# End of a layer in a two-layer hybrid trunk: squares of two of three token chunks added by TensorE, a new order of sums and norms, stores in halves

## Chip, cores and metric

The kernel runs on one core of one Trainium2 chip. The metric is device time of one execution in microseconds (us). The core has five engines that run on their own and meet through semaphores: TensorE (PE, matrix products into the PSUM banks), VectorE (DVE), ScalarE (ACT), GpSimd (POOL) and SyncE (SP, which here only issues transfers).

## The reference, cut to what matters

Two layers run over 1024 prompt tokens and 32 sample tokens. The change lies where a layer ends: the feed-forward result `f` is normed over its 1024 features and added to `x`, and the next layer begins with the norm of the new `x` and its input projection.

```
def rms_norm(x, g):
    xf = x.astype(jnp.float32)
    y = xf * lax.rsqrt(jnp.mean(xf * xf, axis=-1, keepdims=True) + RMS_EPS)
    return (y * g.astype(jnp.float32)).astype(x.dtype)
...
    f = swiglu(rms_norm(x, ng[NORM_FFN_PRE]), w_gu, w_dn)
    x = x + rms_norm(f, ng[NORM_FFN_POST])
    return x, k_keep, v_keep, S_fin, shift_new
...
    P = h @ w_in          # token_mix of the next layer, h = rms_norm(x, ng[NORM_MIX_PRE])
```

## The kernel before, in words

Activations lie with features on the 128 partitions: a tile `[128, 8, 1056]` holds 8 blocks of 128 features for all 1056 tokens. The tokens are worked in three chunks `c` of 352 (0 to 351, 352 to 703, 704 to 1055). `R1` holds `x`; `R2` gathers the feed-forward result and is later reused for squares and for the normed input. Every engine's program is written out by hand, in order; a wait in it holds up whatever is written behind it on that engine. A product of full precision is made of three products of split operands (`WH`, `WL` and `HH`, `HL`), 24 matmuls for one output tile of one chunk.

At the end of a layer each chunk goes through these steps:

- `down(last=True)` on PE makes the last part of the down projection, and `down_sums(c, ...)` on DVE adds it to `R2`, one add for each of 8 blocks. `third_done` tells ACT (`r2_ready`).
- `f_squares(c)` on ACT squares the chunk (2816 elements on each partition) into `SQF`, a single buffer in `TMP`, after waiting until it is free (`fsq_free`). POOL adds the 8 blocks of squares in a tree of three adds into `F_RMS[c]`. `f_stat(c)` on PE, one matmul with a matrix of 1/1024, sums over the partitions into a PSUM bank. The first of them, `f_stat(0)`, stands inside the down projection of chunk 2.
- `root(F_RMS[c], bank)` on ACT makes the reciprocal root out of a logarithm and an exponential (`rms_ready`). `gains_out(c)` multiplies the chunk by the norm's gains, 8 activations.
- `out_normed(c, halves)` on DVE multiplies four blocks by the root and adds them to `R1`, so two `tensor_tensor` for a half. After both halves SP stores the chunk (`x_done`): in layer 0 to `x_spill`, in layer 1 to the output `y`.
- Only behind layer 0: `new_squares(c)` on ACT squares the new `x` in halves, `x_stat(c)` on PE sums them with 8 matmuls, `root(X_RMS[c], ...)` follows, `x_normed` (DVE, 8 operations), `x_high` (ACT, 4 casts) and `x_low` (DVE, 4 subtractions) make the split input, and `opening(c, s)` on PE makes the first two output tiles `s` of the next layer's projection for the chunk, 24 matmuls each. `evac` on ACT copies them out. `lo(0)` and `lo(1)` on DVE finish the split of the two first weight tiles, which `down_split` on ACT begins.

Of the kernel before, what the change touches and what calls it, by code (L numbers as in the profile page):

```python
# [24 lines left out]
ALU = mybir.AluOpType  # L25
# [6 lines left out]
CH = 3  # L32
# [83 lines left out]
def build(nc, io, ctx):  # L116
# [36 lines left out]
    def S(name):  # L153
        if name in ("first_psum", "second_psum"):
            name = "product_of_" + name[:-5] + "_tile"
        elif name.endswith("_psum"):
            name = "product_for_vector" if name in for_vector else "product_for_scalar"
        if name not in sems:
            sems[name] = ctx.enter_context(nc.semaphore(name))
        return sems[name]  # L160

    def give(e, *names):
        for name in names:
            e.sem_inc(S(name), 1)

    def bank(b, a=0, z=512):
        return PS[:, b * 512 + a:b * 512 + z]
# [17 lines left out]
    def chunk(c):  # L185
        return slice(c * CW, (c + 1) * CW)
# [185 lines left out]
    MEM_KV = MIX[:, 14 * ROW + 2560 + MEM:14 * ROW + 2560 + MEM + 4 * 512].rearrange("p (b t) -> p b t", b=4)  # L372


    SQF = tflat[:, 0:DB * CW].rearrange("p (b t) -> p b t", b=DB)
    F_RMS = [SIDE[:, T + 2 + c % 2 * CW:T + 2 + (c % 2 + 1) * CW] for c in range(CH)]
    X_RMS = [SIDE[:, T + 2 + 2 * CW:T + 2 + 3 * CW], tflat[:, DB * CW:(DB + 1) * CW], SIDE[:, T + 2 + 2 * CW:T + 2 + 3 * CW]]
    X_BANK, F_BANKS = 6, (5, 7, 7)
    DOWN_BANKS = [6, 7, 0, 1, 2, 3, 4, 5]


# [21 lines left out]
    def _(e):  # L403
# [12 lines left out]
        for l in range(DEPTH):  # L416
# [141 lines left out]
                w8(0, io["w_in"], l + 1, R0 + 3 * R_WIDTH)  # L558
                w8(1, io["w_in"], l + 1, R0 + 3 * R_WIDTH + P)
            for c in range(CH):  # L560
                e.wait_ge(S("x_done"), 1)
                e.sem_inc(S("x_done"), -1)
                if l < DEPTH - 1:
                    e.dma_start(x_spill[:, :, chunk(c)], R1[:, :, chunk(c)]).then_inc(S("x_spilled"), 16)
                else:
                    e.dma_start(io["y"][:, :, chunk(c)], R1[:, :, chunk(c)]).then_inc(S("y_stored"), 16)
            if l < DEPTH - 1:
                e.wait_ge(S("x_spilled"), 48)
                e.sem_inc(S("x_spilled"), -48)
                give(e, "r1_free")  # L570
        e.wait_ge(S("y_stored"), 48)


    @block.gpsimd
    def _(e):
# [21 lines left out]
        for l in range(DEPTH):  # L597
# [132 lines left out]
            def pool_settled(ins):  # L730

                ins.then_inc(S("pool_done"), 1)
                e.wait_ge(S("pool_done"), 1)
                e.sem_inc(S("pool_done"), -1)

            for c in range(CH):
                e.wait_ge(S("fsq_ready"), 1)
                e.sem_inc(S("fsq_ready"), -1)
                pool_settled(e.tensor_tensor(SQF[:, 0:4, :], SQF[:, 0:4, :], SQF[:, 4:8, :], ALU.add))
                pool_settled(e.tensor_tensor(SQF[:, 0:2, :], SQF[:, 0:2, :], SQF[:, 2:4, :], ALU.add))  # L740
                pool_settled(e.tensor_tensor(F_RMS[c], SQF[:, 0, :], SQF[:, 1, :], ALU.add))
                give(e, "fsq_free", "fsq_sum")
        barrier(e, "pool")


# [1 line left out]
    def _(e):  # L747
        def claim(*banks):
            for b in banks:
                e.wait_ge(S(f"bank{b}"), 1)  # L750
                e.sem_inc(S(f"bank{b}"), -1)  # L751
# [29 lines left out]
                         lambda k, p: H[p][:, k, c * cw:(c + 1) * cw], DB).then_inc(S(name), 1)  # L781

        def x_stat(c):
            claim(X_BANK)
            for h in range(2):
                e.wait_ge(S("xsq_ready"), 1)
                e.sem_inc(S("xsq_ready"), -1)
                for b in range(4 * h, 4 * h + 4):
                    ins = e.matmul(bank(X_BANK, 0, CW), mean, R2[:, b, chunk(c)], start=(b == 0), stop=(b == DB - 1))
            ins.then_inc(S("var_psum"), 1)  # L790

        def f_stat(c):
            e.wait_ge(S("fsq_sum"), 1)
            e.sem_inc(S("fsq_sum"), -1)
            claim(F_BANKS[c])
            e.matmul(bank(F_BANKS[c], 0, CW), mean, F_RMS[c], start=True, stop=True).then_inc(S("var_psum"), 1)

        def opening(c, s):

            if c == 0:  # L800
                e.wait_ge(S(f"w_ready{s}"), 1)
                e.sem_inc(S(f"w_ready{s}"), -1)
            claim(3 * s + c)
            for k in range(DB):
                if s == 0 and k % 2 == 0:
                    e.wait_ge(S("h_ready"), 1)
                    e.sem_inc(S("h_ready"), -1)
                for w, h in ((WH, HH), (WL, HH), (WH, HL)):
                    ins = e.matmul(bank(3 * s + c, 0, CW), w[:, s, k * P:(k + 1) * P], h[:, k, chunk(c)],
                                   start=(k == 0 and w is WH and h is HH), stop=(k == DB - 1 and h is HL))  # L810
            ins.then_inc(S(("first_psum", "second_psum")[s]), 1)
# [5 lines left out]
        for l in range(DEPTH):  # L817
            if l == 0:
                opening(0, 0)
                x_stat(1)  # L820
            else:
                x_stat(1)
                opening(0, 0)
            opening(0, 1)
            opening(1, 0)
            x_stat(2)
            opening(1, 1)
            opening(2, 0)
            opening(2, 1)
# [674 lines left out]
                gate_up()  # L1504
            down(last=True)
            f_stat(1)
            if l < DEPTH - 1:
                x_stat(0)
            f_stat(2)
        barrier(e, "pe")  # L1510


# [2 lines left out]
    def _(e):  # L1515
# [49 lines left out]
        for b in range(8):  # L1565
            give(e, f"bank{b}")

        give(e, "sq_free", "sq_free", "ot_free", "sc_free", "sc_free", "fsq_free")
        roots_ahead()
        split(0)  # L1570
        split(1)
        for l in range(DEPTH):
            PRM = PRMS[:, l * PRM_COLS:(l + 1) * PRM_COLS]
            vec = lambda at, n, j: PRM[:, at + 4 * n + j:at + 4 * n + j + 1]
            if l == 0:
                for c in range(CH):
                    e.wait_ge(S(f"x_full{c}"), 16)
                    e.sem_inc(S(f"x_full{c}"), -16)
                    x_squares(c, 0)
                    x_squares(c, 1)  # L1580
                    root(X_RMS[c], X_BANK)
                    x_high(c, 0, 1, 2, 3)

            def raw(m=P):
# [144 lines left out]
            def settled(ins):  # L1729

                ins.then_inc(S("act_done"), 1)
                e.wait_ge(S("act_done"), 1)
                e.sem_inc(S("act_done"), -1)
# [512 lines left out]
            def f_squares(c):  # L2246
                e.wait_ge(S("r2_ready"), 1)
                e.sem_inc(S("r2_ready"), -1)
                e.wait_ge(S("fsq_free"), 1)
                e.sem_inc(S("fsq_free"), -1)  # L2250
                settled(e.activation(SQF, R2[:, :, chunk(c)], ACT.Square))
                give(e, "fsq_ready")

            def gains_out(c):
                for b in range(DB):
# [22 lines left out]
            f_squares(1)  # L2278
            root(F_RMS[0], F_BANKS[0])
            gains_out(1)  # L2280
            root(F_RMS[1], F_BANKS[1])
            new_squares(0)
            f_squares(2)
            down_split(0)
            down_split(1)
            if l < DEPTH - 1:
                root(X_RMS[0], X_BANK)
                new_squares(1)
                x_high(0, 0, 1, 2, 3)
            gains_out(2)  # L2290
            root(F_RMS[2], F_BANKS[2])
            if l < DEPTH - 1:
                root(X_RMS[1], X_BANK)
                x_high(1, 0, 1, 2, 3)
                new_squares(2)
                root(X_RMS[2], X_BANK)
                x_high(2, 0, 1, 2, 3)
        barrier(e, "act")

# [2 lines left out]
    def _(e):  # L2302
# [35 lines left out]
        for l in range(DEPTH):  # L2338
# [693 lines left out]
            def third_done():  # L3032

                settled(e.memset(ST[:, 0:1], 0.0))
                give(e, "r2_ready")

            def out_normed(c, *halves):
                for h in halves:
                    if h == 0:
                        wait_for("rms_ready")  # L3040
                        wait_for("gained")
                    b = slice(4 * h, 4 * h + 4)
                    r1, r2 = R1[:, b, chunk(c)], R2[:, b, chunk(c)]
                    settled(e.tensor_tensor(r2, r2, F_RMS[c].unsqueeze(1).broadcast_to([P, 4, CW]), ALU.mult))
                    settled(e.tensor_tensor(r1, r1, r2, ALU.add))  # L3045
                    if l < DEPTH - 1:
                        give(e, "r1_ready")
                if 1 in halves:
                    give(e, "x_done")

            half(0)
# [4 lines left out]
            third_done()  # L3056
            down_sums(2, *range(4))
            out_normed(0, 0)
            down_sums(2, 4, 5)
            out_normed(0, 1)  # L3060
            down_sums(2, 6, 7)
            third_done()
            out_normed(1, 0, 1)
            if l < DEPTH - 1:
                NEXT = PRMS[:, (l + 1) * PRM_COLS:(l + 2) * PRM_COLS]
                lo(0)
                lo(1)
                x_normed(NEXT, 0, 0, 1, 2, 3)
                x_low(0, 0, 1, 2, 3)
                out_normed(2, 0, 1)  # L3070
                for c in (1, 2):
                    x_normed(NEXT, c, 0, 1, 2, 3)
                    x_low(c, 0, 1, 2, 3)
            else:
                out_normed(2, 0, 1)
# [53 lines left out]
```

## Time and profile before

| what | value |
|---|---|
| median of 3 runs | 4000.9 us (3997.28 to 4009.68) |
| profiled execution, its own time | 3997.58 us |
| its span, first to last instruction | 3995.6 us |
| mean granted TensorE clock | 0.934 |
| PE busy | 3551.0 us (89%) |
| DVE busy | 1765.8 us (44%) |
| ACT busy | 1300.1 us (33%) |
| POOL busy | 162.7 us (4%) |

The profile is one execution; all places are in us from the start of its span. Shares of busy time are means over the whole span: the two stretches that the change touches (about 1958 to 2050, and 3937 to the end) are read by themselves. A matmul of 352 columns with plain float32 operands shows as two records.

### The profile page before, as it was taken

The page shows a single profiled execution, that of the slowest core. Times are in us where ns is not written, and L with a number is a line of the kernel's source. Part 1 is how long each engine was busy: PE and PEld are TensorE (multiplying, and loading weights), DVE is VectorE, ACT ScalarE, POOL GpSimd, SP SyncE. Part 2 cuts the span into 40 slices and gives each one's busy share as a digit, 9 for nine tenths or more (in the row PEclk, how much of TensorE's full clock was granted, in tenths as well). Part 3 has the DMA queues.
Part 4 walks back from the last instruction along what each step waited for, and adds up shares of the span by engine and source line. Part 5 has one row for each costly group of instructions (what it writes and reads, how often), then busy time and mean ns, then how long its engine had stood idle before and what let it go on. Part 6 is the DMA issues. An engine that isn't in the chain of part 4 may idle for free. (4 is left out here: it accounts for less than half of the span.)

```text
span 3995.6 us, 84425 instructions
## 1 busy us (share of the span) xinstructions
PE 3551.0 (89%) x32662; PEld 3280.0 (82%) x32662; DVE 1765.8 (44%) x2693; ACT 1300.1 (33%) x2505; POOL 162.7 (4%) x188
## 2 busy tenths in 40 slices
PE   6999689869888999999889976998689799999996
PEld 5988367758878999999879864777588699999996
DVE  3254456524554343333443534555345633333334
ACT  3344445323452111111333434443235521111113
POOL 0010000000100000000200100000001000000002
PEclk8999789969999999999989987999799999999998
DMA  2221210117631111111121222001276211111111
GB/s 86 61 70 66 88 45 27 70 39 264 214 124 32 48 43 46 42 52 43 47 70 57 65 68 97 21 26 73 74 249 233 80 43 42 47 47 42 47 47 54
DMA packets 240704, 298.79 MB, mean 75 GB/s; under 512 B 26616, under 2 KB 195952, under 8 KB 239504
## 3 DMA queue, kind: packets, MB, share of 16 engines
q1 hardware_dynamic: 224368, 227.83, 18.0%
q0 software_dynamic: 16032, 66.75, 4.4%
q8 instruction: 209, 3.42, 0.4%
q14 instruction: 95, 0.78, 0.1%
HBM read 228.91 MB, written 65.63 MB: 74 GB/s over the span
## 5 line engine op out<-in xcount | busy, mean ns | idle before, releaser
L767 PE MATMUL PS<-HH,WH 128*128 128x352 f32 (+2 forms) x3584 | 1190.9, 332 | 66.7 <-PEq L751 66.1
L767 PE MATMUL PS<-HH,WL 128*128 128x352 f32 (+2 forms) x3584 | 1164.0, 325 | 0.0
L767 PE MATMUL PS<-HL,WH 128*128 128x352 f32 (+2 forms) x3584 | 1162.6, 324 | 0.0
L767 PEld LDWEIGHTS PS<-HH,WH 128*128 128x128 f32 x3584 | 684.7, 191 | 84.7 <-issue 81.0
L767 PEld LDWEIGHTS PS<-HH,WL 128*128 128x128 f32 x3584 | 684.7, 191 | 2.9 <-issue 0.6
L767 PEld LDWEIGHTS PS<-HL,WH 128*128 128x128 f32 x3584 | 682.4, 190 | 0.0
L2307 DVE TENSOR_TENSOR WL<-WRAW,WH 128x1024 fp32r<-128x1024 f32 x192 | 236.8, 1234 | 672.6 <-DVEq L2306 672.6
L1517 ACT CAST WH<-WRAW 128x1024 fp32r<-128x1024 f32 x216 | 226.3, 1049 | 631.1 <-ACTq L1526 585.1
L1487 PE MATMUL PS<-GH,WH 128*128 128x352 f32 x1056 | 340.2, 322 | 0.0
L1487 PE MATMUL PS<-GL,WH 128*128 128x352 f32 x1056 | 339.5, 322 | 0.0
L1487 PE MATMUL PS<-GH,WL 128*128 128x352 f32 x1056 | 339.5, 322 | 0.0
L3017 DVE TENSOR_TENSOR R<-R,PS 128x352 f32<-128x352 f32 x432 | 199.9, 517 | 145.4 <-DVEq L3011 145.1
L1517 ACT COPY MIX<-PS 128x512 f32<-128x512 f32 (+3 forms) x250 | 130.5, 525 | 345.7 <-ACTq L1737 199.2
L1487 PEld LDWEIGHTS PS<-GH,WL 128*128 128x128 f32 x1056 | 198.3, 188 | 0.2
L1487 PEld LDWEIGHTS PS<-GH,WH 128*128 128x128 f32 x1056 | 198.3, 188 | 0.2
L1487 PEld LDWEIGHTS PS<-GL,WH 128*128 128x128 f32 x1056 | 198.3, 188 | 0.0
L2194 ACT ACTIVATE TMP<-PS 128x352 f32<-128x352 f32 x132 | 61.3, 465 | 400.1 <-ACTq L2193 400.0
L2969 DVE TENSOR_TENSOR TMP<-TMP,PS 128x352 f32<-128x352 f32 x132 | 68.8, 521 | 275.1 <-DVEq L2965 275.1
L2545 DVE COPY_PREDICATED TMP<-CST,PS 128x512 f32<-128x512 uint32 (+1 forms) x162 | 109.8, 696 | 127.1 <-DVEq L2516 127.0
L1517 ACT COPY TMP<-PS 128x256 f32<-128x256 f32 (+2 forms) x252 | 104.4, 444 | 159.9 <-ACTq L1737 138.3
L1517 ACT CAST GH<-TMP 128x352 fp32r<-128x352 f32 x132 | 63.8, 485 | 255.4 <-ACTq L2206 255.4
L1517 ACT COPY R<-PS 128x384 f32<-128x384 f32 (+3 forms) x166 | 73.4, 442 | 186.8 <-ACTq L1534 111.0
(324 smaller groups left out, 4870.9 us busy)
## 6 DMA issues: line engine op xcount, KB each, us to landing
WRAW<-in_w_gate_up SPq DMA_DIRECT2D x88, 512.0 KB, 3.7
W<-split_dram SPq DMA_DIRECT2D x48, 512.0 KB, 4.5
WRAW<-in_w_down SPq DMA_DIRECT2D x44, 512.0 KB, 3.4
WH<-split_dram SPq DMA_DIRECT2D x40, 512.0 KB, 3.7
WL<-split_dram SPq DMA_DIRECT2D x40, 512.0 KB, 4.6
WRAW<-in_w_in SPq DMA_DIRECT2D x38, 512.0 KB, 3.8
raw_dram<-MIX SPq DMA_DIRECT2D x24, 528.0 KB, 2.6
R<-raw_dram SPq DMA_DIRECT2D x24, 512.0 KB, 4.6
```

The costliest lines, as they stand in the source:

```text
L767: ins = e.matmul(out, lhs(k, wp), rhs(k, xp), start=first, stop=(k == n - 1 and xp == 1))
L1487: ins = e.matmul(bank(b, 0, CW), w[:, k, m * P:(m + 1) * P], g[:, k, chunk(c)], start=(k == 0 and w is WH and g is GH), stop=(k == 1 and g ...
L1517: return e.copy(dst, src)
L2194: e.activation(TMP[:, 0, chunk(c)], bank(c, 0, CW), ACT.Silu).then_inc(S("act_done"), 1)
L2307: e.tensor_tensor(WL[:, slot, :], WRAW[:, slot, :], WH[:, slot, :].bitcast(F32), ALU.subtract).then_inc(S("dve_done"), 1)
L2545: e.copy_predicated(x[:, 0:n, :], bits(m).unsqueeze(1).broadcast_to([P, n, CHUNK]), bank(b, 0, n * CHUNK).rearrange("p (g t) -> p g t", t= ...
L2969: e.tensor_tensor(TMP[:, 1, chunk(c)], TMP[:, 0, chunk(c)], bank(3 + c, 0, CW), ALU.mult).then_inc(S("dve_done"), 1)
L3017: e.tensor_tensor(R2[:, m, chunk(c)], R2[:, m, chunk(c)], bank(b, 0, CW), ALU.add).then_inc(S(f"bank{b}"), 1)
```

## The change

For chunks 1 and 2 the tree of adds on POOL is gone: each chunk has a buffer of squares of its own, in `MIX`, and `f_stat(c)` sums the 8 blocks by 8 matmuls into one PSUM bank. Chunk 0 keeps POOL's tree. The wait for the single buffer is gone. DVE makes the whole of chunk 2's down sums before the second half of chunk 0's output norm; the output norm of chunk 2 stands ahead of the next layer's norm of chunk 0. ACT squares chunk 2 ahead of the second root. PE makes `f_stat(2)` ahead of `x_stat(0)`, and `x_stat(2)` ahead of the first opening. Stores go by halves of a chunk (four blocks). Some roots and sums have other buffers and banks.

```
-    SQF = tflat[:, 0:DB * CW].rearrange("p (b t) -> p b t", b=DB)
+    SQF = [MIX[:, DB * T + c * DB * CW:DB * T + (c + 1) * DB * CW].rearrange("p (b t) -> p b t", b=DB) for c in range(CH)]
-    X_BANK, F_BANKS = 6, (5, 7, 7)
+    X_BANKS, F_BANKS = (6, 7, 6), (5, 7, 5)
...
             for c in range(CH):
+                for b in (slice(0, 4), slice(4, 8)):
+                    e.wait_ge(S("x_done"), 1)
...
+                        e.dma_start(x_spill[:, b, chunk(c)], R1[:, b, chunk(c)]).then_inc(S("x_spilled"), 16)
...
         def f_stat(c):
-            e.wait_ge(S("fsq_sum"), 1)
-            e.sem_inc(S("fsq_sum"), -1)
+            name = "fsq_sum" if c == 0 else "fsq_whole"
+            e.wait_ge(S(name), 1)
+            e.sem_inc(S(name), -1)
             claim(F_BANKS[c])
-            e.matmul(bank(F_BANKS[c], 0, CW), mean, F_RMS[c], start=True, stop=True).then_inc(S("var_psum"), 1)
+            rows = [F_RMS[0]] if c == 0 else [SQF[c][:, b, :] for b in range(DB)]
+            for n, row in enumerate(rows):
+                ins = e.matmul(bank(F_BANKS[c], 0, CW), mean, row, start=(n == 0), stop=(n == len(rows) - 1))
+            ins.then_inc(S("var_psum"), 1)
...
             else:
                 x_stat(1)
+                x_stat(2)
                 opening(0, 0)
             opening(0, 1)
             opening(1, 0)
-            x_stat(2)
+            if l == 0:
+                x_stat(2)
...
             f_stat(1)
+            f_stat(2)
             if l < DEPTH - 1:
                 x_stat(0)
-            f_stat(2)
...
             f_squares(1)
             root(F_RMS[0], F_BANKS[0])
             gains_out(1)
+            f_squares(2)
             root(F_RMS[1], F_BANKS[1])
             new_squares(0)
-            f_squares(2)
+            gains_out(2)
             down_split(0)
             down_split(1)
...
             down_sums(2, *range(4))
             out_normed(0, 0)
-            down_sums(2, 4, 5)
+            down_sums(2, *range(4, 8))
+            third_done()
             out_normed(0, 1)
-            down_sums(2, 6, 7)
-            third_done()
             out_normed(1, 0, 1)
             if l < DEPTH - 1:
                 NEXT = PRMS[:, (l + 1) * PRM_COLS:(l + 2) * PRM_COLS]
                 lo(0)
                 lo(1)
-                x_normed(NEXT, 0, 0, 1, 2, 3)
-                x_low(0, 0, 1, 2, 3)
                 out_normed(2, 0, 1)
-                for c in (1, 2):
+                for c in range(CH):
                     x_normed(NEXT, c, 0, 1, 2, 3)
                     x_low(c, 0, 1, 2, 3)
```

On ACT, at the end of layer 0, the order before is this (L2251 is `f_squares`, L2257 `gains_out`, L1551 and L1555 the two steps of `root`, L1546 `new_squares`, L1517 a copy or cast):

```order
L2251 ACTIVATE TMP<-R 128x2816
L1551 ACTIVATE SIDE<-PS,CST 128x352
L1555 ACTIVATE SIDE<-SIDE 128x352
L2257 ACTIVATE R<-R,PRMS 128x352 x8
L1551 ACTIVATE SIDE<-PS,CST 128x352
L1555 ACTIVATE SIDE<-SIDE 128x352
L1546 ACTIVATE R<-R 128x4x352 x2
L2251 ACTIVATE TMP<-R 128x2816
L1517 CAST WH<-WRAW 128x1024 x2
L1551 ACTIVATE SIDE<-PS,CST 128x352
L1555 ACTIVATE SIDE<-SIDE 128x352
L1546 ACTIVATE R<-R 128x4x352 x2
```

The same place of the changed kernel, from `f_squares(1)` on (the lines' numbers are higher by 5 to 7):

```order
L2256 ACTIVATE MIX<-R 128x2816
L1558 ACTIVATE SIDE<-PS,CST 128x352
L1562 ACTIVATE SIDE<-SIDE 128x352
L2262 ACTIVATE R<-R,PRMS 128x352 x8
L2256 ACTIVATE MIX<-R 128x2816
L1558 ACTIVATE SIDE<-PS,CST 128x352
L1562 ACTIVATE SIDE<-SIDE 128x352
L1553 ACTIVATE R<-R 128x4x352 x2
L2262 ACTIVATE R<-R,PRMS 128x352 x8
L1524 CAST WH<-WRAW 128x1024 x2
L1558 ACTIVATE TMP<-PS,CST 128x352
L1562 ACTIVATE TMP<-TMP 128x352
```

Chunk 2's squares moved ahead of the second root, and chunk 2's gains and third output root moved ahead of the next layer's first root.

On PE, the end of layer 0 before, from the last matmul of the down projection (L1487) on, with `f_stat` (L796), `x_stat` (L789) and the first opening (L809):

```order
L1487 MATMUL PS<-GL,WH 128x352
L796 MATMUL PS<-SIDE,CST 128x352
L789 MATMUL PS<-R,CST 128x352 x8
L796 MATMUL PS<-SIDE,CST 128x352
L789 MATMUL PS<-R,CST 128x352 x8
L809 MATMUL PS<-HH,WH 128x352
```

And of the changed kernel:

```order
L1494 MATMUL PS<-GL,WH 128x352
L800 MATMUL PS<-MIX,CST 128x352 x16
L790 MATMUL PS<-R,CST 128x352 x24
L814 MATMUL PS<-HH,WH 128x352
L814 MATMUL PS<-HH,WL 128x352
```

Both output sums of 8 matmuls now stand ahead of all three sums of the next norm, and all of these ahead of the first opening.

On DVE, from the second half of chunk 1's output norm (L3044, L3045) on, before: `lo` (L2307), `x_normed` (L2319), `x_low` (L2327).

```order
L3044 TENSOR_TENSOR R<-R,SIDE 128x4x352
L3045 TENSOR_TENSOR R<-R 128x4x352
L2307 TENSOR_TENSOR WL<-WRAW,WH 128x1024 x2
L2319 SCALAR_TENSOR_TENSOR R<-R,PRMS,SIDE 128x352 x8
L2327 TENSOR_TENSOR HL<-R,HH 128x2x352 x4
L3044 TENSOR_TENSOR R<-R,SIDE 128x4x352
L3045 TENSOR_TENSOR R<-R 128x4x352
```

And of the changed kernel:

```order
L3048 TENSOR_TENSOR R<-R,SIDE 128x4x352
L3049 TENSOR_TENSOR R<-R 128x4x352
L2311 TENSOR_TENSOR WL<-WRAW,WH 128x1024 x2
L3048 TENSOR_TENSOR R<-R,TMP 128x4x352
L3049 TENSOR_TENSOR R<-R 128x4x352
L3048 TENSOR_TENSOR R<-R,TMP 128x4x352
L3049 TENSOR_TENSOR R<-R 128x4x352
L2323 SCALAR_TENSOR_TENSOR R<-R,PRMS,SIDE 128x352 x8
L2331 TENSOR_TENSOR HL<-R,HH 128x2x352 x4
```

The output norm of chunk 2, four operations, passed the next layer's norm and split of chunk 0, twelve operations.

## Rows read from the trace of the kernel before

**Rows 1.** PE by stretch (us from start): length, busy (instructions), granted clock, DMA share, GB/s.

```profile
1983.00:1985.00 2.00, 1.51 (x2) 0.50 0.00 0
2009.00:2017.00 8.00, 7.64 (x49) 1.00 0.00 0
2017.00:2026.00 9.00, 0.00 (x0) 0.67 0.43 160
2060.00:2150.00 90.00, 89.44 (x560) 0.99 0.21 60
```

**Rows 2.** Timeline of POOL, layer 0's end: start, length, operation, idle before.

```profile
1974.20 3.23 POOL L739 TENSOR_TENSOR TMP<-TMP 128x1408 f32<-128x1408 f32 x1 [3.10 <-POOLq L738]
...
1980.62 2.09 POOL L741 TENSOR_TENSOR SIDE<-TMP 128x352 f32<-128x352 f32 x1 [0.18 <-POOLq L734]
```

**Rows 3.** Timeline of ACT, layer 0's end and layer 1's start.

```profile
1962.01 2.55 ACT L2251 ACTIVATE TMP<-R 128x2816 f32<-128x2816 f32 x1 [5.80 <-ACTq L2250]
...
1971.35 2.56 ACT L2251 ACTIVATE TMP<-R 128x2816 f32<-128x2816 f32 x1 [2.65 <-ACTq L2250]
1974.19 0.56 ACT L1551 ACTIVATE SIDE<-PS,CST 128x352 f32<-128x352 f32 x1 [0.28 <-ACTq L1550]
...
1975.34 3.93 ACT L2257 ACTIVATE R<-R,PRMS 128x352 f32<-128x352 f32 x8
...
1986.01 2.63 ACT L1546 ACTIVATE R<-R 128x1408 f32<-128x1408 f32 x2
1988.54 2.54 ACT L2251 ACTIVATE TMP<-R 128x2816 f32<-128x2816 f32 x1
1991.44 2.00 ACT L1517 CAST WH<-WRAW 128x1024 fp32r<-128x1024 f32 x2 [0.36 <-ACTq L1526]
...
2049.04 0.52 ACT L1517 COPY SIDE<-PS 128x320 f32<-128x320 f32 x2 [4.73 <-ACTq L1534]
```

**Rows 4.** Timeline of DVE, the same stretch.

```profile
1961.58 0.06 DVE L3034 MEMSET ST<- 128x1 f32 x1
...
1969.01 0.06 DVE L3034 MEMSET ST<- 128x1 f32 x1
...
1974.50 0.52 DVE L3030 TENSOR_TENSOR R<-R,PS 128x352 f32<-128x352 f32 x1 [0.43 <-DVEq L2516]
1975.69 3.22 DVE L3044 TENSOR_TENSOR R<-R,SIDE 128x1408 f32<-128x1408 f32 x1 [0.68 <-DVEq L2516]
...
2001.65 1.22 DVE L2307 TENSOR_TENSOR WL<-WRAW,WH 128x1024 fp32r<-128x1024 f32 x1 [0.44 <-DVEq L2306]
...
2013.52 1.62 DVE L3044 TENSOR_TENSOR R<-R,SIDE 128x1408 f32<-128x1408 f32 x1 [2.93 <-DVEq L2516]
...
2018.93 1.62 DVE L3045 TENSOR_TENSOR R<-R 128x1408 f32<-128x1408 f32 x1
...
2038.28 4.06 DVE L2319 SCALAR_TENSOR_TENSOR R<-R,PRMS,SIDE 128x352 f32<-128x352 f32 x8 [10.01 <-DVEq L2316]
2042.25 3.29 DVE L2327 TENSOR_TENSOR HL<-R,HH 128x704 fp32r<-128x704 f32 x4
```

**Rows 5.** Timeline of PE: output sums (L796), sums of the next norm (L789).

```profile
1971.60 0.83 PE L796 MATMUL PS<-SIDE,CST 128*128 128x352 f32 x2 [1.31 <-PEq L751]
1983.21 1.51 PE L796 MATMUL PS<-SIDE,CST 128*128 128x352 f32 x2 [5.05 <-PEq L751]
2001.93 7.08 PE L789 MATMUL PS<-R,CST 128*128 128x352 f32 x16
2031.86 4.89 PE L789 MATMUL PS<-R,CST 128*128 128x352 f32 x16
```

**Rows 6.** Timeline of DVE, layer 1's end: first and last output-norm operations.

```profile
3954.35 3.22 DVE L3044 TENSOR_TENSOR R<-R,SIDE 128x1408 f32<-128x1408 f32 x1 [0.68 <-DVEq L2516]
...
3987.89 1.62 DVE L3045 TENSOR_TENSOR R<-R 128x1408 f32<-128x1408 f32 x1
```

**Rows 7.** Half a microsecond within the last store, columns as in rows 1.

```profile
3992.00:3992.50 0.50, 0.00 (x0) 0.50 1.07 400
```

More of the change, by code:

```diff
@@ L372, in build @@
     MEM_KV = MIX[:, 14 * ROW + 2560 + MEM:14 * ROW + 2560 + MEM + 4 * 512].rearrange("p (b t) -> p b t", b=4)
-    SQF = tflat[:, 0:DB * CW].rearrange("p (b t) -> p b t", b=DB)
-    F_RMS = [SIDE[:, T + 2 + c % 2 * CW:T + 2 + (c % 2 + 1) * CW] for c in range(CH)]
+    SQF = [MIX[:, DB * T + c * DB * CW:DB * T + (c + 1) * DB * CW].rearrange("p (b t) -> p b t", b=DB) for c in range(CH)]
+    F_RMS = [SIDE[:, T + 2:T + 2 + CW], SIDE[:, T + 2 + CW:T + 2 + 2 * CW], tflat[:, 0:CW]]
     X_RMS = [SIDE[:, T + 2 + 2 * CW:T + 2 + 3 * CW], tflat[:, DB * CW:(DB + 1) * CW], SIDE[:, T + 2 + 2 * CW:T + 2 + 3 * CW]]
-    X_BANK, F_BANKS = 6, (5, 7, 7)
+    X_BANKS, F_BANKS = (6, 7, 6), (5, 7, 5)
     DOWN_BANKS = [6, 7, 0, 1, 2, 3, 4, 5]
@@ L560, in _ @@
             for c in range(CH):
[L561 to L566, printed above, removed]
+                for b in (slice(0, 4), slice(4, 8)):
+                    e.wait_ge(S("x_done"), 1)
+                    e.sem_inc(S("x_done"), -1)
+                    if l < DEPTH - 1:
+                        e.dma_start(x_spill[:, b, chunk(c)], R1[:, b, chunk(c)]).then_inc(S("x_spilled"), 16)
+                    else:
+                        e.dma_start(io["y"][:, b, chunk(c)], R1[:, b, chunk(c)]).then_inc(S("y_stored"), 16)
             if l < DEPTH - 1:
-                e.wait_ge(S("x_spilled"), 48)
-                e.sem_inc(S("x_spilled"), -48)
+                e.wait_ge(S("x_spilled"), 96)
+                e.sem_inc(S("x_spilled"), -96)
                 give(e, "r1_free")
-        e.wait_ge(S("y_stored"), 48)
+        e.wait_ge(S("y_stored"), 96)
     @block.gpsimd
@@ L734, in pool_settled @@
                 e.sem_inc(S("pool_done"), -1)
[L736 to L742, printed above, removed]
+            e.wait_ge(S("fsq_ready"), 1)
+            e.sem_inc(S("fsq_ready"), -1)
+            sq = SQF[0]
+            pool_settled(e.tensor_tensor(sq[:, 0:4, :], sq[:, 0:4, :], sq[:, 4:8, :], ALU.add))
+            pool_settled(e.tensor_tensor(sq[:, 0:2, :], sq[:, 0:2, :], sq[:, 2:4, :], ALU.add))
+            pool_settled(e.tensor_tensor(F_RMS[0], sq[:, 0, :], sq[:, 1, :], ALU.add))
+            give(e, "fsq_sum")
         barrier(e, "pool")
@@ L783, in x_stat @@
         def x_stat(c):
-            claim(X_BANK)
+            claim(X_BANKS[c])
             for h in range(2):
@@ L788, in x_stat @@
                 for b in range(4 * h, 4 * h + 4):
-                    ins = e.matmul(bank(X_BANK, 0, CW), mean, R2[:, b, chunk(c)], start=(b == 0), stop=(b == DB - 1))
+                    ins = e.matmul(bank(X_BANKS[c], 0, CW), mean, R2[:, b, chunk(c)], start=(b == 0), stop=(b == DB - 1))
             ins.then_inc(S("var_psum"), 1)
         def f_stat(c):
-            e.wait_ge(S("fsq_sum"), 1)
-            e.sem_inc(S("fsq_sum"), -1)
+            name = "fsq_sum" if c == 0 else "fsq_whole"
+            e.wait_ge(S(name), 1)
+            e.sem_inc(S(name), -1)
             claim(F_BANKS[c])
-            e.matmul(bank(F_BANKS[c], 0, CW), mean, F_RMS[c], start=True, stop=True).then_inc(S("var_psum"), 1)
+            rows = [F_RMS[0]] if c == 0 else [SQF[c][:, b, :] for b in range(DB)]
+            for n, row in enumerate(rows):
+                ins = e.matmul(bank(F_BANKS[c], 0, CW), mean, row, start=(n == 0), stop=(n == len(rows) - 1))
+            ins.then_inc(S("var_psum"), 1)
         def opening(c, s):
@@ L822, in _ @@
                 x_stat(1)
+                x_stat(2)
                 opening(0, 0)
@@ L825, in _ @@
             opening(1, 0)
-            x_stat(2)
+            if l == 0:
+                x_stat(2)
             opening(1, 1)
@@ L1506, in _ @@
             f_stat(1)
+            f_stat(2)
             if l < DEPTH - 1:
                 x_stat(0)
-            f_stat(2)
         barrier(e, "pe")
@@ L1566, in _ @@
             give(e, f"bank{b}")
-        give(e, "sq_free", "sq_free", "ot_free", "sc_free", "sc_free", "fsq_free")
+        give(e, "sq_free", "sq_free", "ot_free", "sc_free", "sc_free")
         roots_ahead()
@@ L1580, in _ @@
                     x_squares(c, 1)
-                    root(X_RMS[c], X_BANK)
+                    root(X_RMS[c], X_BANKS[c])
                     x_high(c, 0, 1, 2, 3)
@@ L2248, in f_squares @@
                 e.sem_inc(S("r2_ready"), -1)
[L2249 to L2252, printed above, removed]
+                settled(e.activation(SQF[c], R2[:, :, chunk(c)], ACT.Square))
+                give(e, "fsq_ready" if c == 0 else "fsq_whole")
             def gains_out(c):
@@ L2280, in _ @@
             gains_out(1)
+            f_squares(2)
             root(F_RMS[1], F_BANKS[1])
             new_squares(0)
-            f_squares(2)
+            gains_out(2)
             down_split(0)
             down_split(1)
[L2286 to L2290, printed above, removed]
             root(F_RMS[2], F_BANKS[2])
             if l < DEPTH - 1:
-                root(X_RMS[1], X_BANK)
+                root(X_RMS[0], X_BANKS[0])
+                new_squares(1)
+                new_squares(2)
+                x_high(0, 0, 1, 2, 3)
+                root(X_RMS[1], X_BANKS[1])
                 x_high(1, 0, 1, 2, 3)
-                new_squares(2)
-                root(X_RMS[2], X_BANK)
+                root(X_RMS[2], X_BANKS[2])
                 x_high(2, 0, 1, 2, 3)
@@ L3047, in out_normed @@
                         give(e, "r1_ready")
-                if 1 in halves:
                     give(e, "x_done")
@@ L3058, in _ @@
             out_normed(0, 0)
-            down_sums(2, 4, 5)
+            down_sums(2, *range(4, 8))
+            third_done()
             out_normed(0, 1)
-            down_sums(2, 6, 7)
-            third_done()
             out_normed(1, 0, 1)
@@ L3067, in _ @@
                 lo(1)
-                x_normed(NEXT, 0, 0, 1, 2, 3)
-                x_low(0, 0, 1, 2, 3)
                 out_normed(2, 0, 1)
-                for c in (1, 2):
+                for c in range(CH):
                     x_normed(NEXT, c, 0, 1, 2, 3)
```

## The prediction

> **What bounds the kernel now.** I read the stretches of TensorE first. From 2060 on it is busy 89.44 of 90 us at full clock, so what comes earlier at the start of layer 1 comes earlier to the end, as long as TensorE stays the bound; just ahead of that it stands idle, 9 us from 2017 to 2026 alone [rows 1]. So the end of layer 0 and the start of layer 1 are a chain of small steps on four engines, and so is the end of layer 1, behind which nothing runs but the last store. I followed that chain in the timelines of the single engines. The reader is to see how late chunk 2 is: its squares start at 1988.54 [rows 3], its output norm runs from 2013.52 to 2020.55 [rows 4], the sum for its next norm starts at 2031.86, behind an opening [rows 5], its next norm at 2038.28 after 10.01 us without work for VectorE [rows 4], and the copy of its first opened tile at 2049.04 [rows 3]. I take this last place as the end of the first stretch. In layer 1 the end is VectorE's last addition, 3987.89 + 1.62 = 3989.51 [rows 6], and 6.1 us of store up to the end of the span at 3995.6.
>
> **Layer 0, step by step.** Each new place is the place of the releaser plus a duration from a row.
>
> Chunk 1's squares waited 2.65 us for the one buffer and started at 1971.35 [rows 3]. With their own buffer they follow the memset that ends chunk 1's sums (1969.01 [rows 4]) by 0.43, as in chunk 0 (1961.58 [rows 4] to 1962.01 [rows 3]): 1969.44 to 1972.0. The sum of chunk 0 on TensorE stays where it is, ending at 1971.60 + 0.83 = 1972.43 [rows 5], and the first root, which started at 1974.19 behind those squares, starts near 1972.6. A root takes 1.25 (1974.19 to just behind 1975.34 [rows 3]); so 1973.85, then chunk 1's gains, 3.95, to 1977.8.
>
> VectorE finishes block 3 of chunk 2 at 1975.02 [rows 4] and begins chunk 0's output norm at 1975.25. The first operation took 3.22 there while POOL added (1974.20 on [rows 2]), and 1.62 where POOL was at rest [rows 4]. POOL's second tree is gone, so I take a half from 2013.52 to 2020.55, where two halves took 7.03 [rows 4]: 3.4, to 1978.65. Four adds at about 0.45 (0.52 for one alone [rows 4]) follow, to 1980.8. Chunk 2's squares start at 1981.2, not 1988.54, and end at 1983.75.
>
> TensorE ends the down projection at 1983.21 - 5.05 = 1978.16 [rows 5]. Eight matmuls from the squares' buffer do not occur before; the nearest rows are the sums of the next norm, also eight matmuls of 352 columns: 4.89 at full clock, 7.08 where the clock was half at first [rows 5]. Half throughout would be twice 4.7, 9.4. The first output sum stands right behind the projection at full clock, so I take 4.89: to 1983.0. The second waits for chunk 2's squares, 1.1 us idle, little less than the 1.31 after which one matmul still took 0.83 [rows 5]; again 4.89, 1984.1 to 1989.0. Before, POOL's tree alone took from 1974.20 to 1982.71 for chunk 1 [rows 2].
>
> ScalarE then has no pause: second root to 1985.3, squares of the new chunk 0 (2.63) to 1987.9, gains of chunk 2 (3.95) to 1991.85, two casts (0.36 + 2.00 [rows 3]) to 1994.2, third root to 1995.5. Here the stall goes: VectorE, done with chunk 0 at 1984.7 and with chunk 1 (1985.55 + 7.03) at 1992.6, waits for the casts, makes its two splits (1.22 and a gap of 0.44 each [rows 4]) to 1996.4, and begins chunk 2's output norm at 1996.8 instead of 2013.52; it ends at 2003.85.
>
> ScalarE makes the next norm's first root to 1996.7 and chunk 1's new squares to 1999.3; TensorE, idle for about 4 us after chunk 0's sum (1989.0 to 1993.9), begins chunk 1's sum at 1998.1. I take the 7.08 of the same sum before [rows 5]: 2005.2. Chunk 2's new squares end at 2005.5, its sum at 2009.9, the gate for the first opening now. The other gate, the first quarter of VectorE's split input, is open by 2009.2: 2003.85, 0.45, 4.06 for the norm, a quarter of 3.29 [rows 4]. So the first opening goes from near 2008.6 to 2009.9, a loss of 1.3 that costs nothing, since the openings of chunk 1 waited until 2026 anyhow.
>
> From there work is packed. Two openings took 7.64 [rows 1], 3.82 each; chunks 0 and 1 last until 2025.2. VectorE meanwhile makes norm and split of chunks 1 and 2 at 0.45 + 4.06 + 3.2 each: chunk 2's first quarter is ready at 2024.6, just in time. Chunk 2's first opening ends at 2029.0 and its copy is at 2029.1, where it was 2049.04: **19.9 us**. The weights that SP loads behind its wait for the spills come earlier too: the last half is handed over at 2003.85 instead of 2020.55, the load is needed at 2029.8. If that cover of some 20 us were gone, each microsecond would count in full.
>
> **Layer 1.** The steps lie 3954.35 - 1975.69 = 1978.66 later [rows 4, 6]. Chunk 2's squares end at 3962.4, the output sums at 3961.6 and 3967.7, the second root at 3963.95; chunk 1's output norm runs from 3964.2 to 3971.2, the third root is there by 3969.1, and chunk 2's norm ends at 3978.5, 11.0 ahead of 3989.51. The store of a chunk is 128 x 8 x 352 x 4 = 1.44 MB, 3.6 us at the 400 GB/s of [rows 7]; half of it is still to go at VectorE's end, the first half has left 3.5 us before. That saves 1.8: **12.8 us** in all.
>
> A page speaks against halves: the Trainium skill (DMA: Bandwidth & Descriptors, Anatomy of one DMA) gives each transfer a fixed part of some 2.0 us besides its bytes at 436 GB/s, so that two halves pay it twice. By that estimate the last half takes 2.0 + 1.65 us against 2.0 + 3.3, and the sum would be 0.15 us higher; the trace agrees on a part that does not shrink, 6.1 less 3.6. No run here shows a half store yet.
>
> Bounds of that store: nothing saved (+1.8, if both halves land together) and 1.8. Bounds of the sums on TensorE: all at 4.89 the first opening would be limited by the split input at 2009.2, 0.7 sooner; chunk 1's and 2's sums both at 9.4 put it to 2016.9, 7 later. The other edits (banks, buffers in other tiles, no wait for a free buffer, the halved spill) I put at nothing: an operation on 352 columns does not depend on its tile in these rows, and SP has no other work there; at most 1 us either way.
>
> **Sum.** 3997.6 (the profiled execution's own time) - 19.9 - 12.8 = 3964.9. The median of the runs shown is 3.3 above that execution; going a third of the way, I predict 3966.
>
> **Rivals.** *TensorE at half clock in both sums' stretches.* The clock does fall in such pauses: 1.51 for one matmul at 1983.21, at the 1.2 GHz level, after 5.05 us idle [rows 1, 5]. If it fell in the change's new pauses too and all sums took 9.4: output sums to 1987.5 and 1996.9, the three others to 2025.1, the first opening 15.2 later; in layer 1 the last norm starts at 3977.1, 5.7 later. 3964.9 + 20.9 = 3985.8. Against it: no pause of over 1.4 us stands ahead of the output sums, and the sum at 2001.93 rose to full clock within itself (7.08, not 9.4 [rows 5]). The Trainium skill (TensorE: Matmul & The Clock Gate, Part 1) says that the array's default is the throttled state and that activity releases it; by that rule only the sums after pauses pay, and the trace agrees.
>
> *Slower: the half clock holds through the openings.* They stand in the same queue, behind all sums. Five openings at twice 3.82 add 19.1: 4004.9, and every further tile of 72 matmuls 11.5. It turns into a loss once about three openings run at half clock besides all the sums. Against it: from 2009 to 2017 two openings ran at 1.00 [rows 1].
>
> *The next layer swallows its part.* If the loads behind the spills, or VectorE's work on the first tiles, set the start of the long products, only layer 1's 12.8 stays: 3984.8. Against it: TensorE is full from 2060 on [rows 1], and everything between the copy at 2049.04 and there hangs on that copy.
>
> *The change does not do what it says.* ScalarE, in order, is then late by as much as POOL was, and the time is 3997.6. It would need 33 us of new waits; ScalarE's work between 1969 and 1996 holds only the 4 us that VectorE waits and splits.
>
> **Chances.** Forecast 0.79; half clock 0.08; swallowed 0.06; slower 0.03; nothing 0.04. The forecast's own range is 3960 to 3974: the bounds above and the runs' spread. For 8 in 10 I reach a little into the rivals: 3958 to 3979. Within 0.3% means 12 us here, what a measurement of this kernel can hardly tell from no change. Faster by more: the forecast, the swallowed case and half of the first rival, 0.89; within: 0.08; slower by more: 0.03.
>
> **What the profile will show.** If right: no POOL adds for chunks 1 and 2; sixteen matmuls behind the down projection in about 11 us at clock 1.00; the first operation of the output norm at 1.6, not 3.2; chunk 2's output norm from 1997; the first opening near 2010 and from there no idle TensorE of more than 2 us until 2029; VectorE's last addition near 3978 and the end under 4.5 us behind it. Wrong, if the sums on TensorE show 9 us, if ScalarE's third root comes after 1998, or if the first opening starts after 2017.

## The result and the profile after

The changed kernel takes 3960.27 us (median of 4 runs, 3954.13 to 3967.17) against 3999.09 us for the kernel before (4 runs). The medians differ by 38.8 us. The ratio on record, worked out from the runs of both, is 0.989, 95% interval 0.9873 to 0.9907, so the change is faster by some 39 to 44 us; the forecast of 3966 lay 35 us below the median of 4000.9 that it went from. Five more runs gave a ratio of 0.9894 (0.9877 to 0.9911). The profiled execution takes 3954.13 us.

The trace is best read in four parts. The first end goes from the memset behind chunk 0's sums of layer 0 (1961.58 in [rows 4]) to the copy of chunk 2's first opened tile (2049.04 in [rows 3]), the second from the same memset of layer 1 to the end of the span. Ahead of the first end, and between the two, both kernels do the same work in the same order; only the bank of a sum at the start of layer 0 differs. The lengths in this table are differences of such places in the two traces.

| part, us | before | after | difference |
|---|---|---|---|
| up to layer 0's end | 1961.58 | 1955.06 | -6.52 |
| layer 0's end | 87.46 | 66.63 | -20.83 (19.9 forecast) |
| layer 1 between the ends | 1891.18 | 1888.92 | -2.26 |
| layer 1's end | 55.38 | 41.89 | -13.49 (12.8 forecast) |

The first and the third row of this one pair are not a result: the runs below show how much executions of one kernel differ there.

Timeline of VectorE in the changed kernel, layer 0's end, answering to [rows 4]. In brackets stand the idle time ahead of an operation and what ended it; DVEq, ACTq and PEq are the engines' own sequencers, in which the waits stand:

```profile
1955.06 0.06 DVE L3038 MEMSET ST<- 128x1 f32 x1
...
1968.25 1.62 DVE L3048 TENSOR_TENSOR R<-R,SIDE 128x1408 f32<-128x1408 f32 x1
...
1978.54 1.63 DVE L3048 TENSOR_TENSOR R<-R,SIDE 128x1408 f32<-128x1408 f32 x1 [0.98 <-DVEq L2520]
...
1989.56 1.63 DVE L3048 TENSOR_TENSOR R<-R,TMP 128x1408 f32<-128x1408 f32 x1 [0.56 <-DVEq L2520]
...
1997.14 4.05 DVE L2323 SCALAR_TENSOR_TENSOR R<-R,PRMS,SIDE 128x352 f32<-128x352 f32 x8 [0.46 <-DVEq L2320]
2001.12 3.29 DVE L2331 TENSOR_TENSOR HL<-R,HH 128x704 fp32r<-128x704 f32 x4
2004.33 4.04 DVE L2323 SCALAR_TENSOR_TENSOR R<-R,PRMS,TMP 128x352 f32<-128x352 f32 x8
2008.30 3.28 DVE L2331 TENSOR_TENSOR HL<-R,HH 128x704 fp32r<-128x704 f32 x4
2011.51 4.05 DVE L2323 SCALAR_TENSOR_TENSOR R<-R,PRMS,SIDE 128x352 f32<-128x352 f32 x8
```

The first operation of the output norm takes 1.62, not 3.22; chunk 2's norm starts 34.5 behind the memset, where it started 51.9 behind it; and behind the operation at 1978.54 no pause exceeds 0.56 up to the end of chunk 2's split at 2018.7. The 10 us pause ahead of chunk 2's next norm is gone. From 1978.54 on VectorE sets the pace of this stretch; ahead of that it still waits for TensorE's down projection.

Timelines of ScalarE and of TensorE in the changed kernel, same stretch, answering to [rows 3, 5]:

```profile
1962.84 2.55 ACT L2256 ACTIVATE MIX<-R 128x2816 f32<-128x2816 f32 x1 [0.74 <-ACTq L2255]
...
1974.20 2.55 ACT L2256 ACTIVATE MIX<-R 128x2816 f32<-128x2816 f32 x1 [3.23 <-ACTq L2255]
1977.03 0.56 ACT L1558 ACTIVATE SIDE<-PS,CST 128x352 f32<-128x352 f32 x1 [0.28 <-ACTq L1557]
...
1986.43 0.54 ACT L1558 ACTIVATE TMP<-PS,CST 128x352 f32<-128x352 f32 x1
...
2021.69 0.52 ACT L1524 COPY SIDE<-PS 128x320 f32<-128x320 f32 x2 [4.15 <-ACTq L1541]
```

```profile
1971.32 4.89 PE L800 MATMUL PS<-MIX,CST 128*128 128x352 f32 x16
1977.17 4.97 PE L800 MATMUL PS<-MIX,CST 128*128 128x352 f32 x16 [0.96 <-PEq L752]
1981.98 4.90 PE L790 MATMUL PS<-R,CST 128*128 128x352 f32 x16
1990.22 11.40 PE L790 MATMUL PS<-R,CST 128*128 128x352 f32 x32 [3.34 <-PEq L788]
```

Both output sums of eight matmuls run at full clock, at 4.9 each. The two sums of the next norm behind the pause of 3.34 take 11.4 together, 1.6 more than twice 4.9, and the granted clock is near its lower level at their start. PE by stretch, columns as in [rows 1]:

```profile
1990.20:1994.00 3.80, 3.78 (x7) 0.55 0.00 0
1994.00:1998.00 4.00, 4.00 (x15) 1.00 0.51 188
```

The memset behind chunk 0's sums and the last operation of VectorE in layer 1, answering to [rows 6]:

```profile
3910.61 0.06 DVE L3038 MEMSET ST<- 128x1 f32 x1
...
3946.92 1.62 DVE L3049 TENSOR_TENSOR R<-R 128x1408 f32<-128x1408 f32 x1
```

The latter ends 3.9 ahead of the end of the span (3952.5); before, 6.1.

### The profile page after: what moved, and what is told of

Read it like the earlier page. It is cut to its first block and busy times, and to the rows that moved or that the text cites. A ratio compares the mean times of both kernels' runs of the same rounds, so it can differ in the third digit from the quotient of the medians.

```text
span 3952.5 us, 84510 instructions
## 1 busy us (share of the span) xinstructions
PE 3549.4 (90%) x32718; PEld 3277.7 (83%) x32718; DVE 1754.3 (44%) x2693; ACT 1300.6 (33%) x2505; POOL 130.5 (3%) x176
```

## Experiments

**The kernel before again**, for the parts that no edit touched.

> The kernel before, unchanged. Between the two profiles 6.5 us of the difference lie ahead of the end of layer 0 and 2.3 us between the two ends, where both kernels have the same instructions. Theory (these 8.8 us are what one execution differs from the next by, not the change): this profile reaches the memset behind chunk 0's sums of layer 0 at a place that differs from 1961.58 by several us, the length from the opened tile's copy to the same memset of layer 1 differs from 1891.2 by some us, and the time stands at 1.000 +- 0.002. Rival (the change makes the unchanged stretches shorter, by the bank of a sum at the start or the place of a buffer): the memset stands within 1 us of 1961.6 and the second stretch within 1 us of 1891.2.

Ratio 1.0001 (0.9979 to 1.0024). The 27 runs of before beside this and the next three kernels went from 3984.68 to 4022.62 us. The profile reaches the memset at 1954.59, 7.0 sooner than the first one, and layer 1 between the ends takes 1899.1, 7.9 longer. The two ends take 87.52 and 55.39, within 0.1 of the first. So the ends repeat; the other parts don't, and a single pair of profiles can't be subtracted there.

**Stores of whole chunks** (the edit on SP and the matching counts):

```
-                for b in (slice(0, 4), slice(4, 8)):
...
+                e.dma_start(x_spill[:, :, chunk(c)], R1[:, :, chunk(c)]).then_inc(S("x_spilled"), 16)
```

> The changed kernel with stores of whole chunks. Theory: from VectorE's last addition to the end of the span 6.1 us instead of the 4.0 of the changed kernel, nothing else in the two ends moves (70.1 us from chunk 0's sums to the copy of chunk 2's opened tile in layer 0): some 2 us slower than the changed kernel, ratio to before about 0.990. Rival (the spill in halves lets the next layer's weights come sooner and counts in layer 0): the layer 0 stretch grows by 1 us or more as well.

Ratio 0.992 (0.9895 to 0.9945). Layer 0's end 66.72, layer 1's 43.77; from VectorE's last addition to the end 6.12. The half store is worth 1.9 us, all at the very end. The spill in halves is worth nothing.

**POOL adds again, new order kept:**

```
-            rows = [F_RMS[0]] if c == 0 else [SQF[c][:, b, :] for b in range(DB)]
+            rows = [F_RMS[c]]
...
+            for c in range(CH):
+                e.wait_ge(S("fsq_ready"), 1)
```

> The changed kernel, but POOL adds the squares of all chunks again, with the new order and a buffer for each chunk. Theory (order and sums share the gain, the order having most of it in layer 0): the output norm's first operation takes 3.2 us again, chunk 2's output norm starts 3 to 4 us later in layer 0 and 6 us later in layer 1, so about 9 us slower than the changed kernel, ratio 0.992. Rival (the sums on TensorE are the whole gain): both ends are back near the lengths of before, 91 and 55 us, ratio 1.0. Rival (the order is the whole gain): within 2 us of the changed kernel.

Ratio 0.9937 (0.9913 to 0.9961). Layer 0's end 73.29, layer 1's 47.20: 6.7 and 5.3 longer than in the changed kernel. Chunk 1's output norm in this kernel, on VectorE, against POOL's adds for chunk 2:

```profile
1992.54 3.53 DVE L3048 TENSOR_TENSOR R<-R,SIDE 128x1408 f32<-128x1408 f32 x1 [0.97 <-DVEq L2520]
1996.22 2.86 DVE L3049 TENSOR_TENSOR R<-R 128x1408 f32<-128x1408 f32 x1
```

```profile
1991.05 3.54 POOL L741 TENSOR_TENSOR MIX<-MIX 128x1408 f32<-128x1408 f32 x1 [4.62 <-POOLq L739]
1994.77 2.83 POOL L742 TENSOR_TENSOR MIX<-MIX 128x704 f32<-128x704 f32 x1 [0.18 <-POOLq L735]
```

VectorE's 1.62 becomes 3.53 and 2.86 while POOL adds. The first ends 1.5 behind the end of POOL's first add (1994.59), the second (1999.08) 1.5 behind the end of its second (1997.60). So the two seem to take turns. GpSimd's adds suffer too: the second one takes 2.83 here, and 1.71 for chunk 0, where VectorE's adds beside it take one operand from PSUM. The direction and the contention are as expected, and neither rival holds; layer 0's part was expected at 3 to 4 and is 6.7, layer 1's at 6 and is 5.3.

**Only the sums on TensorE, old order** (`f_stat`, buffers and POOL's part as in the change, chunk 2's buffer in `TMP`):

```
+            rows = [F_RMS[0]] if c == 0 else [SQF[c][:, b, :] for b in range(DB)]
```

> The kernel before with the sums of chunks 1 and 2 on TensorE, buffers of their own (chunk 2's in TMP), and nothing else changed: old order, whole stores. Theory: layer 1's end is shorter by about 9.6 us, since VectorE's last addition comes that much sooner; layer 0's by only about 7 of the 20.8, since chunk 2's output norm still stands behind chunk 0's next norm and its next sum behind an opening: ratio about 0.996. Rival (the sums are the whole gain): 20 us in layer 0, ratio 0.991. Rival (only the order counts): ratio 1.000.

Ratio 0.996 (0.9939 to 0.9981). The ends take 79.38 and 47.31, each 8.1 shorter than before: 7 and 9.6 were expected. In layer 0 VectorE still waits ahead of chunk 2's output norm:

```profile
2001.18 1.62 DVE L3046 TENSOR_TENSOR R<-R,TMP 128x1408 f32<-128x1408 f32 x1 [2.94 <-DVEq L2518]
```

So the sums alone give 8.1 of the 20.8 us in layer 0. The order with POOL's sums gave 14.2 of them; the two overlap a little.

**The changed kernel again.**

> The changed kernel again. Up to here the two ends of the trace are 20.8 and 13.5 us shorter than before, 34.3 in all, and they repeat to 0.1 us, while the unchanged stretches differ by up to 13 us between executions. Theory (only the ends count): ratio 34.3 / 4001 below one, 0.9914, with the ends at 66.6 and 41.9 us again. Rival (the first four runs' 0.989 holds something that the ends don't show): 0.989 or below.

Ratio 0.9894 (0.9877 to 0.9911), 42 us, not the 34 of the ends. The ends are 67.10 and 41.94, within 0.5 of the first profile. The theory that only the ends count, 0.9914, fell just outside the interval.

**Chunk 2's next sum behind an opening again:**

```
             else:
                 x_stat(1)
-                x_stat(2)
                 opening(0, 0)
             opening(0, 1)
             opening(1, 0)
-            if l == 0:
-                x_stat(2)
+            x_stat(2)
```

> The changed kernel with the sum of chunk 2's next norm behind the first opening of chunk 1 again, as before. Theory: VectorE, which works without pause up to chunk 2's next norm in the changed kernel, gets a pause of some 8 us ahead of it (the sum starts near the end of that opening, takes 5 us, the root 1.3), so layer 0's end is 74 to 76 us instead of 66.6 and layer 1's stays at 41.9; ratio 0.9935. Rival (the place of this sum doesn't count, since the first opening is held up by it as much as it gains): 66 to 67 us.

Ratio 0.9922 (0.9907 to 0.9938). Layer 0's end 78.53, 11.9 longer (7.4 to 9.4 expected), layer 1's 41.93. The wait ahead of chunk 2's next norm is back on VectorE:

```profile
2025.45 4.06 DVE L2321 SCALAR_TENSOR_TENSOR R<-R,PRMS,SIDE 128x352 f32<-128x352 f32 x8 [11.23 <-DVEq L2318]
```

This one move in TensorE's order carries more than half of layer 0's gain, as long as the others stand.

**Chunk 2's last down sums late again** (`down_sums(2, 4, 5)`, `out_normed(0, 1)`, `down_sums(2, 6, 7)` as before).

> The changed kernel with the last down sums of chunk 2 behind the second half of chunk 0's output norm again, in the pieces of before. Theory: chunk 2's squares start some 3.6 us later, ScalarE makes the second root behind them, and VectorE waits that much longer: layer 0's end 70.3, layer 1's 45.5 us instead of 66.6 and 41.9. Rival (the pause is taken up by the wait for the second root that stands there anyhow): both ends within 1 us of the changed kernel.

One run, 3969.9 us. Ends 71.27 and 45.98, 4.6 and 4.1 longer (3.7 and 3.6 expected). Chunk 1's output norm waits for the second root, which ScalarE makes at 1987.75, behind chunk 2's squares:

```profile
1989.25 1.63 DVE L3048 TENSOR_TENSOR R<-R,SIDE 128x1408 f32<-128x1408 f32 x1 [4.62 <-DVEq L2520]
```

**Moved on:** chunk 0's output sum one block later, one weight split earlier, the last half stored in quarters.

```
-                        if by_block and i == 3:
+                        if by_block and i == 5:
...
             out_normed(0, 1)
+            if l < DEPTH - 1:
+                lo(0)
             out_normed(1, 0, 1)
```

> The changed kernel with three further moves: chunk 0's output sum one block later in the down projection (behind block 2 instead of 1), the first of the two weight splits ahead of chunk 1's output norm (its cast ahead of chunk 2's squares), and the last half of the last chunk added and stored in two quarters. Theory (VectorE's chain bounds both ends): TensorE's wait of 1.2 us for POOL goes, about 0.9 us in each end; the split fills a pause of 1.0, about 0.5 in layer 0; the quarter saves 0.7 at the end: ends of 65.2 and 40.3 us, 3 us below the changed kernel, ratio to before 0.9907. Rival (the pauses only move on): ends as in the changed kernel.

Ratio 0.989 (0.9872 to 0.9908), which its runs can't tell from the changed kernel's. Its ends are 65.37 and 40.39, 1.3 and 1.5 shorter, as expected. It is the shortest version by the ends. The 0.9907 expected lies inside the interval too.

**Where the other 7 to 8 us are.** In the three profiles of before the part up to layer 0's end takes 1957.1 in the mean, in the two of the changed kernel 1957.0. Layer 1 between the ends takes 1895.0 and 1884.7. Over all 13 traces it takes 1891.2 to 1902.3 in the five with the old number of matmuls on TensorE ahead of it, and 1880.4 to 1891.0 in the eight with 14 more. Cutting all traces at ScalarE's table loads showed one stretch of layer 1 that no edit touches, 73.2 us before and 66.1 after. PE by stretch, columns as in [rows 1], in the kernel before (the whole, and its last part) and in the changed kernel:

```profile
2579.45:2652.67 73.22, 67.08 (x1581) 0.92 0.11 35
2635.00:2652.67 17.67, 14.50 (x286) 0.68 0.01 3
```

```profile
2554.06:2620.14 66.08, 62.43 (x1593) 1.00 0.12 39
```

Before, the granted clock falls to its lower level in the last part; after, it stays at 1.00 all through. Just ahead of the low part TensorE stands still for 1.49 us, and the profile names nothing that it waited for ("issue"); timeline of PE in the kernel before:

```profile
2640.07 0.21 PE L1089 MATMUL PS<-R,TMP 64*64 64x64 f32 x1 [1.49 <-issue]
```

The pause stood in every kernel with the old number of matmuls on TensorE up to there, and in none of those with 14 more. Two kernels test whether that number matters. The first is the kernel before with 14 unused matmuls.

> The kernel before with 14 matmuls more on TensorE at the start of layer 1, between two openings, where it stands idle for 9 us; their sums go to a free bank and are not used. So TensorE's program of layer 1 lies behind as many more instructions as in the changed kernel, while the ends keep the old work. The question is one stretch of layer 1 that no edit touched, between two table loads of ScalarE: 73.2, 72.3 and 73.0 us in the three kernels with the old number of matmuls, with a pause of 1.5 to 1.8 us of TensorE 60 us in, for which the profile names no releaser, and half clock behind it; 65.9 to 66.4 us without that pause in the seven kernels with 14 more. Theory (where TensorE's program lies decides that pause): 66 us here too, no such pause, and the time about 5 to 8 us below before, ratio 0.998 to 0.9985, layer 0's end within 3 us of 87.5. Rival (the pause hangs on when the work comes, and the earlier ends moved it): 73 us and ratio 1.000.

The edit, at the start of layer 1:

```
             opening(0, 1)
+            if l > 0:
+                claim(7)
+                for n in range(14):
+                    ins = e.matmul(bank(7, 0, CW), mean, R1[:, 0, chunk(0)], start=True, stop=True)
+                ins.then_inc(S("bank7"), 1)
             opening(1, 0)
```

Ratio 0.9977 (0.9956 to 0.9997): the kernel before becomes some 9 us faster (1 to 18) by 14 matmuls that nobody uses. Layer 0's end is 85.53, 1.9 shorter than 87.46. There is no pause in the stretch:

```profile
2573.87:2639.53 65.66, 61.86 (x1585) 1.00 0.13 39
```

The second is the changed kernel with 14 left out, so that layer 1 works on other numbers.

> The changed kernel with 14 of the 24 matmuls of the next norm's sums at layer 0's end left out (7 of 8 blocks for chunks 1 and 2, so layer 1 works on other numbers), so that TensorE's program of layer 1 lies where it lay before, with the short ends. Theory (the program's place decides): the stretch is 73 us again with the pause of 1.5 us or more, ratio 0.991 or above, though the sums left out make layer 0's end no longer than 66.7. Rival (timing decides): 66 us, ratio 0.989.

The edit leaves out 7 of 8 blocks of two sums:

```
+                blocks = range(7, 8) if short else range(4 * h, 4 * h + 4)
...
+                x_stat(1, short=True)
+                x_stat(2, short=True)
```

The stretch is long again, with the pause, though it starts 602 us behind the memset of layer 0's end, nearly as early as in the changed kernel (599):

```profile
2567.76:2640.29 72.53, 66.97 (x1585) 0.93 0.11 35
```

```profile
2627.84 0.21 PE L1099 MATMUL PS<-R,TMP 64*64 64x64 f32 x1 [1.22 <-issue]
```

Its ratio, 0.9893 (0.9865 to 0.9922), is open to both expectations. Layer 0's end was 69.23 and not 66.7 or less: without those matmuls the granted clock was 0.50 from 2012.80 to 2018.40, over the start of the openings.

Last, the kernel before a third time.

> The kernel before once more, for the same stretch: by the theory 72 to 73 us and the pause again, as in the two executions so far; by the rival that the pause comes by chance in a single execution, 66 us in some of them.

One run, 3993.88 us: the stretch 71.0, the pause 1.77. The ends 86.78 and 55.42. In three executions of before, then, the pause stood each time; with the 14 unused matmuls and in the changed kernel it was absent. The number of matmuls ahead makes it come and go. When the work comes does not: counted from that memset the stretch starts at 618 in before and 602 with the 14 left out, both with the pause, and at 613 with the 14 unused ones, between them, without it.

The traces say more than the word "issue". In all five traces with the pause, 22084 records of TensorE's matmuls stand ahead of it. In all 13 traces together TensorE has 65 pauses of over 0.9 us without a named releaser, and each ends 1.2 to 1.6 us behind the end of a 16 KB packet of the transfer queue that the page lists as "instruction" (before: packet from 2637.56 to 2638.81, TensorE goes on at 2640.07). Of 245 waits as long with a named releaser, in the same parts of the traces, only 2 end so. So these pauses go with the delivery of instructions. No run changed that delivery by itself.

The number ahead is not all, though. Two pauses of the same kind (1.6 to 2.1 us) stand in the matching stretch of layer 0 in two kernels, the one with POOL's adds in the new order and the one with 14 matmuls left out (72.9 and 73.5 us against 65.6 to 66.3 in all others). Their edits lie behind that stretch, so the number ahead is the same there. Why these two have them is open.

## Why the prediction was right and where it was wrong

**Right, by its own steps.** Chunk 2's squares were put 19.6 behind the memset and came 19.1 behind it; the two output sums on TensorE at 16.6 and 22.5 (16.3 and 22.1), 4.89 each (4.89 and 4.97); chunk 2's output norm at 35.2 (34.5); the first opening at 48.3 (47.1, 2002.15 in the trace); the copy at 67.5 (66.6). The first operation of chunk 0's output norm takes 1.62 without POOL's adds beside it, as the row of 3.22 said it would. One stall that it foresaw did not come: ScalarE's casts, which were to hold VectorE by a microsecond, do not, and VectorE has continuous work from chunk 1's output norm on.

**Terms off in size.** Layer 0's end: 19.9 forecast, 20.8 measured, with chunk 2's squares 0.5 sooner and without the wait for ScalarE's casts. Layer 1's end: 12.8 and 13.5; of it the half store gave 2.1 in the profiles of before and after (1.9 against whole stores alone) where 1.8 was put. The estimate by the Trainium skill (DMA: Bandwidth & Descriptors, Anatomy of one DMA), 1.65 saved, lies further off than the row's, and the measurement decides; the page gives that fit for transfers that GpSimd issues, and here SyncE issues them. Against that, chunk 1's and 2's next sums were put at 12.0 and took 11.4.

**What failed.** The sum, 3997.6 - 19.9 - 12.8, has no term for layer 1 between the two ends. "What comes earlier at the start of layer 1 comes earlier to the end" holds, but layer 1 was taken to keep its length, with no reason given, and the 14 more matmuls on TensorE were priced only where they run. The runs showed instead that with 14 more matmuls ahead of layer 1 a pause of 1.2 to 1.8 us, and the half clock behind it, vanish in one stretch some 600 us later: 73.2 us to 66.1. That is the missing 7.1: 34.3 in the ends and 7.1 make 41.4, beside 39 to 44 measured. The banks, buffers and the halved spill that the prediction put "at nothing" are not what failed as far as the runs show: the spill was worth 0.1 us, and no run tried the others alone. That the number of matmuls ahead makes this pause come and go is shown both ways, by the 14 added to the old kernel and the 14 taken from the new one. That TensorE waits in it for instructions fits every such pause in the traces, but no run tested it alone.

**The rivals.** Half clock in the output sums did not come: 4.89 and 4.97. It came where the prediction had put it, in the sum of the next norm behind a pause (0.55 from 1990.20 to 1994.00). The next layer swallowed nothing: it became shorter. The opening's delay behind chunk 2's sum cost nothing, and the run with that sum late shows that its place is worth 11.9.

**The range** reached down to 3958, which allowed for the terms of the two ends and the spread of the runs, but not for layer 1 between them. The median of 3960.27 lies inside it; the ratio of 0.989, taken of the 4000.9 from which the forecast went, gives 3956.9, just below it.

## What to carry to other kernels

Where several engines hand a chunk around, find the engine that has the most work in the stretch and put the others' order so that it never waits: here one sum moved ahead of an opening was worth 11.9 us with the other moves in place, while replacing POOL's adds brought 8 by itself. Adds on GpSimd and two-operand adds on VectorE slow each other down: 1.62 became 3.53 on VectorE, and 1.71 became 2.83 on GpSimd. Before a difference of a few tenths of a per cent is put down to an edit, cut the traces into parts, run the old kernel again, and compare the parts that the edit didn't touch: one of them can have changed for a reason of its own. Here the number of instructions ahead changed one.

## What the runs showed of the hardware

Fourteen unused matmuls made a kernel of 4000 us faster by 0.23% (0.03% to 0.44%). Against the three profiles of before, 1.3 to 2.0 us of it came at their own place, where TensorE had been idle, and 5.4 to 7.6 us in a stretch some 600 us behind it, through a pause without a named releaser and the half clock that followed. Every such pause of over 0.9 us, 65 in 13 traces, ended 1.2 to 1.6 us behind the end of a 16 KB instruction packet. One of them, 2.4 to 4.0 us long, stands behind 23955 records of TensorE's matmuls in all 13 traces, although in the eight with 14 more matmuls ahead (28 records) the work has come 28 records less far there. So this pause belongs to a place in TensorE's program and not to the work that stands there. What decides whether a place has a pause is open.
